# Group norm statistics from transposed y and ScalarE running sums; six depthwise-convolution taps moved behind the last turn

## The reference, cut to what matters

```
y = y * silu(z)                                        # 256 tokens x 256 channels of the group
yg = y * rsqrt(mean(y * y over the group's 256 channels) + 1e-6)
out = (yg * norm_g) @ out_w                            # summed over the groups
```

## Time and profile before

| | us |
|---|---|
| median of 3 runs | 915.81 |
| lowest and highest | 915.27, 915.85 |
| the profiled execution | 916.38 |
| its span in the trace | 914.6 |
| PE busy in the span | 903.7 |
| DVE busy | 757.4 |
| ACT busy | 560.1 |
| POOL busy | 18.3 |

### The profile page before, as it was taken

The page is one execution under the profiler, slowest core; times in us unless marked ns, Lnnn a source line. Parts: engine busy times, 40 slices in busy tenths (PEclk is TensorE's granted clock), DMA queues, the critical chain, the costliest instruction groups (busy, mean ns, idle before and its releaser), DMA issues.

```text
span 914.6 us, 18324 instructions
## 1 busy us (share of the span) xinstructions
PE 903.7 (99%) x6655; PEld 852.1 (93%) x6655; DVE 757.4 (83%) x1381; ACT 560.1 (61%) x954; POOL 18.3 (2%) x30
## 2 busy tenths in 40 slices
PE   9999999999999999999999999999999999999997
PEld 7999989999999999998888888999999999999886
DVE  5999999999999979689888646889979988888543
ACT  5649666776668474567666535579656766656432
POOL 1000000000000000000000000100000000000000
PEclk9999999999999999999999999999999999999999
DMA  9577235635346537537655554455437455555601
GB/s 329 178 269 228 97 116 183 202 128 197 137 163 207 207 94 278 183 117 251 199 186 187 186 185 163 143 179 186 153 132 264 147 195 179 181 180 180 230 1 46
DMA packets 45630, 161.56 MB, mean 177 GB/s; under 512 B 5348, under 2 KB 6024, under 8 KB 45448
## 3 DMA queue, kind: packets, MB, share of 16 engines
q1 hardware_dynamic: 43488, 154.74, 50.2%
q10 hardware_dynamic: 2088, 6.08, 1.8%
HBM read 159.72 MB, written 1.09 MB: 176 GB/s over the span
## 4 chain that ended last, share of the span: by engine, by line
PE 58%; issue 25%; DVE 13%; ACT 2%; DMA 1%; POOL 0%; SPq 0%; DVEq 0%; POOLq 0%; ACTq 0%
PE A L446 8%; PE A L447 7%; PE A L448 7%; PE B L665 5%; DVE w_lo L1347 4%; PE A L475 4%; PE B L475 3%; PE B L446 2%; PE B L447 2%; PE B L448 2%; PE A L477 2%; DVE part L1383 2%; PE B L477 2%; PE B L746 2%; PE A L746 1%
## 5 line engine op out<-in xcount | busy, mean ns | idle before, releaser
L1347 DVE TENSOR_TENSOR w_lo<-raw,w_hi 128x1024 fp32r<-128x1024 f32 x269 | 326.1, 1220 | 66.5 <-ACT w_hi L897 65.0
L897 ACT ACTIVATE w_hi<-raw 128x1024 fp32r<-128x1024 f32 x269 | 280.2, 1052 | 70.2 <-PE A L747 20.9
L446 PE MATMUL A<-h,w_hi 128*128 128x256 f32 x952 | 273.8, 288 | 0.2 <-DVE sc L1961 0.2
L447 PE MATMUL A<-h,w_hi 128*128 128x256 f32 x952 | 269.2, 283 | 0.0
L448 PE MATMUL A<-h,w_lo 128*128 128x256 f32 x952 | 269.2, 283 | 0.0
L446 PEld LDWEIGHTS A<-h,w_hi 128*128 128x128 f32 x952 | 182.1, 191 | 3.2 <-issue 2.6
L447 PEld LDWEIGHTS A<-h,w_hi 128*128 128x128 f32 x952 | 182.3, 192 | 0.1
L448 PEld LDWEIGHTS A<-h,w_lo 128*128 128x128 f32 x952 | 182.1, 191 | 0.0
L446 PE MATMUL B<-h,w_hi 128*128 128x256 f32 x352 | 100.1, 284 | 0.0
L447 PE MATMUL B<-h,w_hi 128*128 128x256 f32 x352 | 99.6, 283 | 0.0
L448 PE MATMUL B<-h,w_lo 128*128 128x256 f32 x352 | 99.6, 283 | 0.0
(11 more groups left out here) (308 smaller groups left out, 1575.5 us busy)
## 6 DMA issues: line engine op xcount, KB each, us to landing
raw<-in_weights_dram SPq DMA_DIRECT2D x289, 512.0 KB, 4.3
csrow<-cs_dram ACTq DMA_DIRECT2D x9, 512.0 KB, 4.5
x<-in_x_dram SPq DMA_DIRECT2D x4, 256.0 KB, 4.7
bd<-in_lru_w_dram ACTq DMA_DIRECT2D x1, 1024.0 KB, 6.2
out_dram<-m_wide SPq DMA_DIRECT2D x3, 256.0 KB, 2.1
raw<-in_weights_dram SPq DMA_DIRECT2D x2, 256.0 KB, 5.3
par<-in_params_dram SPq DMA_DIRECT2D x1, 379.0 KB, 6.8
out_dram<-m_wide ACTq DMA_DIRECT2D x2, 128.0 KB, 2.7
```

What stands on the lines that cost most here:

```text
L446: mm(dst, wh, lo, start=first, stop=False, skip_group_check=free)
L447: mm(dst, wh, hi, start=False, stop=False, skip_group_check=free)
L897: F(w_hi[:, s, :], raw[:, s, :], ACT.Copy).then_inc(hi_ready, 1)
L1347: V.tensor_tensor(w_lo[:, s, :], raw[:, s, :], w_hi[:, s, :].bitcast(F32), ALU.subtract).then_inc(lo_ready, 1)
```

## The change

The sums of squares are made another way. TensorE transposes the four 128 x 128 blocks of `y` into `A[3]` (tokens then on partitions), ScalarE squares each half of 128 x 256 out of PSUM with a running sum along the row (`accum_out`) into the new tile `ysum`, and `y_mean` reads `ysum` in SBUF. In the turns g = 1 to 7 the transposes stand in the middle of the second `out_piece`, after four of its eight matmuls; in the first turn they stand where `y_sums` stood. ScalarE's order changes with it. Three taps each of the channel tiles 0 and 1 (taps 24 to 26) leave the first turn and are made right after the last one. In the first and the last turn `y_mean` now comes ahead of the `w_lo` split beside it.

```diff
-            def y_sums(g):
-                pe.wait_ge(ysq_ready, g + 1)
+            def y_transposes(g):
+                pe.wait_ge(yz_ready, g + 1)
                 for t in range(TT):
                     for c in range(2):
-                        ins = mm(sums[:, t:t + 1], ysq[:, c, t * P:(t + 1) * P], ones[:, 0:1],
-                                 start=c == 0, stop=c == 1)
-                ins.then_inc(sums_ready, 1)
+                        ins = nc.tensor.transpose(A[3][:, t * T + c * P:t * T + (c + 1) * P], y[:, c, t * P:(t + 1) * P],
+                                                  ident)
+                ins.then_inc(yt_ready, 1)
...
-            def out_piece(p, turn, g, c):
+            def out_piece(p, turn, g, c, between=None):
                 native_loaded(p, turn)
                 pe.wait_ge(scale_read, g + 2)
                 for m in range(KD):
+                    if between is not None and m == KD // 2:
+                        y_transposes(between)
...
-            chain = {1: cb, 2: x_transposes, 3: y_products, 4: y_sums, 5: y_scale}
+            chain = {1: cb, 2: x_transposes, 3: y_products, 5: y_scale}
...
-                        out_piece(base + OUT_AT[s // 4], t, g - 1, s // 4)
+                        out_piece(base + OUT_AT[s // 4], t, g - 1, s // 4, g if s == 4 else None)
...
-            first_chain = {1: cb, 3: x_transposes, 5: y_products, 7: y_sums, 8: y_scale}
+            first_chain = {1: cb, 3: x_transposes, 5: y_products, 7: y_transposes, 8: y_scale}
...
             def y_squares(g):
-                act.wait_ge(yz_ready, g + 1)
-                F(ysq[:, :, :], y[:, :, :], ACT.Square).then_inc(ysq_ready, 1)
+                act.wait_ge(yt_ready, g + 1)
+                for t in range(TT):
+                    ins = F(ysq[:, t, :], A[3][:, t * T:(t + 1) * T], ACT.Square, accum_out=ysum[:, t:t + 1])
+                ins.then_inc(sums_ready, 1)
...
                 split(6)
+                act.wait_ge(cb_used, g + 1)
+                first_taps(g + 1, (0, 1))
+                act.wait_ge(yz_ready, g + 1)
+                first_taps(g + 1, (2, 3))
                 y_squares(g)
-                first_taps(g + 1)
...
                     if n == 6:
+                        act.wait_ge(yz_ready, 1)
+                        first_taps(1)
                         y_squares(0)
-                        first_taps(1)
...
-            GLU_TAPS, LOOP_TAPS, LATE_TAPS = range(5), range(5, CONV_K - 4), range(CONV_K - 4, CONV_K)
+            GLU_TAPS, LOOP_TAPS, LATE_TAPS = range(5), range(5, CONV_K - 7), range(CONV_K - 4, CONV_K)
+            LAST_TAPS = range(CONV_K - 7, CONV_K - 4)
...
-                moment_of(g + 2, 2 * P, RMS_EPS).then_inc(mean_ready, 1)
+                moment_of(g + 2, 2 * P, RMS_EPS, ysum[:, :]).then_inc(mean_ready, 1)
...
-                lo()
-                y_mean(g)
+                if looped:
+                    lo()
+                    y_mean(g)
+                else:
+                    y_mean(g)
+                    lo()
...
             group_turn(g, ahead(GATES0, 8), GATES0 + OUT_AT[1] + 1, more=False)
+            late_taps((0, 1), LAST_TAPS)
             for n in range(8, GATE_AT[-1] + 1 - LEAD):
```

More of the change, by code:

```diff
@@ L223, in hybrid_kernel @@
         dt_parts = ysq[:, 0, :]
+        ysum = sb("ysum", [P, TT], scope=s3)
         s3.close()
@@ L340, in hybrid_kernel @@
         dec_ready, m_ready, y_ready, yz_ready = sem("dec_ready"), sem("m_ready"), sem("y_ready"), sem("yz_ready")
-        ysq_ready, first_tap = sem("ysq_ready"), sem("first_tap")
+        yt_ready, first_tap = sem("yt_ready"), sem("first_tap")
         conv_operand_ready, mixed_ready = sem("conv_operand_ready"), sem("mixed_ready")
@@ L690, in _ @@
                 if s in (1, 4):
-                    out_piece(GATES0 + OUT_AT[s // 4], 0, g - 1, s // 4)
+                    out_piece(GATES0 + OUT_AT[s // 4], 0, g - 1, s // 4, g if s == 4 else None)
                 if s in chain:
@@ L965, in ring, with first_taps @@
                 return A[o % 3][:, 0:T]
-            def first_taps(g):
+            def first_taps(g, js=range(4)):
                 act.wait_ge(drained, drained_by(g, 3))
                 dyn = not isinstance(g, int)
-                for j in range(4):
+                for j in js:
                     at = (g * 4 + j) * SSM_K + SSM_K - 1
@@ L1601, in y_normed, with late_taps @@
                 ins.then_inc(scale_read, 1)
-            def late_taps(cs):
+            def late_taps(cs, ks=LATE_TAPS):
                 last = {c: own.value() for c in cs}
-                for k in LATE_TAPS:
+                for k in ks:
                     for c in cs:
```

## The result

| | before | after |
|---|---|---|
| median, us | 915.58 | 916.88 |
| lowest and highest, us | 914.9, 916.03 | 916.31, 917.5 |
| the profiled execution, its span | 916.38, 914.6 | 916.67, 914.9 |

The ratio is 1.0015 (95% interval 1.0009 to 1.0021), from 20 runs of each: the change makes the kernel 1.3 us slower. That is inside the 1.8 us that the prediction called "within 0.2%", and inside its range, but the forecast of -1.84 us has the wrong sign.

What follows compares the result with a forecast made beforehand. The prediction took TensorE as the bound, busy 903.7 of 914.6 us. Loop -2.76, first turn +1.0 and tail -0.08 made -1.84 us, from a median of 915.81 to 914.0 us; range 910.6 to 917.4.

Steps and rivals of the forecast that it cites:

- TensorE's own work, 0.46 us a turn: In every turn, four transposes (0.35 us) replace the sums' matmul group (0.81 us): 0.46 us less, bounds 0.3 to 0.8.
- The squares: ScalarE's two squares per turn, with running sums: 0.75 us for both, bounds 0.5 to 1.5 us.
- rival D: TensorE's clock falls because transposes don't count as activity: +12 us, 926 us; chance 0.02.
- rival B: Slow squares make ScalarE the bound: at 2.0 us for two, +4.1 us, 919.9 us; chance 0.10.
- The first turn, +1.0: ScalarE's squares wait for TensorE's transposes, so the loop begins 1.0 us late; bounds +0.75 to +1.75.
- rival A: ScalarE doesn't hold the first turn: -5.4 us, 910.4 us; 913.1 if only the tail is better; chance 0.19 with better tail.
- The loop, -2.76: In the loop and its first part, six turns (g = 1 to 6) each gain TensorE's 0.46 us: -2.76 us.
- the 27.8: Loop period in us above which the prediction called itself wrong; it expected 27.6.
- Rival C: VectorE or the loads, late by 0.43 us, hold the loop turn: +0.9 us, 916.7 us; chance 0.15.
- The tail, -0.08: Last turn and behind: TensorE's gain goes into waiting at the layer norm's sum behind six taps; -0.08 us, bounds -1.0 to +0.5.

Runs made afterwards that it cites:

- Experiment 3: Changed kernel with the first turn's transposes of y behind the seventh piece instead of the eighth: 914.85 us, ratio 0.9990.
- experiment 6: Changed kernel with the six moved taps back in the first turn: 915.69 us, ratio 1.0001.
- experiment 5: Kernel before the change, with only the six taps moved from the first turn behind the last: 914.86 us, ratio 0.9992.
- six memsets, not counted: Changed kernel with six small VectorE memsets added in the first turn, not raising VectorE's own semaphore: 915.68 us, ratio 1.0002.
- experiment 9: Changed kernel with the first turn's transposes behind the seventh piece and the mean ahead of VectorE's split in every turn: 912.74 us, ratio 0.9967.
- before, late mean: Kernel before the change, with the mean made two taps later in the loop turns: 921.86 us, ratio 1.0065.
- experiments 6 to 8: Changed kernel with the six taps back in the first turn (915.69 us), or six memsets added there, uncounted (915.68 us) or counted by VectorE's semaphore (915.89 us).
- experiment 2: Changed kernel with the mean directly ahead of VectorE's split in the loop turns too: 914.87 us, ratio 0.9991.
- experiment 1: Changed kernel with the mean made between the taps in the loop turns, two taps ahead of VectorE's split: 915.44 us, ratio 0.9998.

## Why the prediction was wrong, by its own steps

**TensorE's own work, 0.46 us a turn: right.** Transposes in the cut `out_piece` take 161.92 - 161.48 = 0.44 us of starts, not 0.35, but what stands behind them starts sooner by about as much; the turn up to the scale is 0.45 us shorter. The squares were inside their bounds: from the first square to the table load 0.85 us, a pair being 0.37 us from start to start (0.75 for two in the prediction). The granted clock stayed at 1.00, so rival D fell; rival B too, with 0.37 us a square.

**The first turn, +1.0: right, +1.02.** Each sign is there: ScalarE's wait of 1.92 us for the transposes, VectorE's of 3.33 for the split, TensorE's of 1.70 for the gate drain and 1.33 for `dec` (forecast 1.5 to 2). With that rival A fell. Experiment 3 moves the one instruction group that was blamed and gets 2.00 us back; experiment 6 shows that the taps have no part in it, though with the old sums they gain 1.15 us (experiment 5). The chain was read rightly. What was not drawn from it is that the cure was one number in a table.

**The loop, -2.76: the step that failed.** In its words: "GpSimd ends at 165.76 and TensorE, 0.46 us earlier, comes to L547 at 165.93 [...]: 0.15 us of slack, no wait." (The two times differ by 0.17.) No wait is printed at L548, but the time is lost behind it, and the period of 28.06 us lies above the 27.8 that the prediction named as the sign of being wrong. Set GpSimd's end against the start of the scale and of the next turn's first matmul, which stands behind the loop's back edge:

| kernel | GpSimd ends | scale starts, later by | next turn's first matmul, later than GpSimd's end by |
|---|---|---|---|
| before | 165.76 | 0.63 | 0.77 |
| before, taps moved | 164.29 | 0.51 | 0.65 |
| mean before split | 221.31 | 0.43 | 0.63 |
| taps back | 166.13 | 0.17 | 0.64 |
| six memsets, not counted | 165.80 | 0.17 | 0.64 |
| experiment 9 | 219.01 | 0.43 | 0.68 |
| after | 166.45 | 0.07 | 0.64 |
| before, late mean | 225.79 | 0.06 | 0.63 |

However the scale comes, the next turn's first matmul starts 0.63 to 0.68 us behind GpSimd's end in seven of these kernels (0.62 to 0.69 in their turns g = 2 to 5), and not sooner; only before, which has time to spare, shows more. The next matmul follows the scale after 0.13 to 0.14 us when nothing holds it, so the scale needs a lead of 0.5 us. Before had 0.63, that is 0.13 us of real slack and not the 0.63 that the rows seemed to show; the change asked for 0.46.

That the back edge has a part in it, the same instructions show where there is no jump back. On the last pass, g = 6, which leaves the loop, the next matmul starts 0.40 us behind GpSimd's end in after (0.39 in before, late mean; 0.41 in taps back), and in the last turn, which is written out, 0.24 us. The reading that fits is that TensorE's sequencer runs ahead of the array, so that its waits and the jump back are normally done before the array gets there, and that a scale which comes late stops it ahead of the jump. No row shows the sequencer itself. The Trainium skill says as much of the running ahead ("TensorE: Matmul & The Clock Gate", Part 2, step ⑤ NX overlap: the sequencer pops the next instruction without waiting for the array to drain). The 0.64 us are measured here; that the stopped sequencer is their cause is argued, not shown.

The second part of the same term: the chain to GpSimd's start should not have moved, and it came 0.12 us later (13.71 us behind the transposes, before 13.59). That is VectorE's 0.27 us in place of 0.16 ahead of y, shown in experiments 6 to 8 to come from there being six instructions fewer in the stream ahead of the loop. Together: 13.71 + 0.85 + 0.64 = 15.20 us from the transposes to the next turn, and before needed 15.22 for TensorE's own work. The period could only stay.

**Rival C** gave 916.7 and the median is 916.88, but its mechanism, "VectorE or the loads late by 0.43 us", is not what happened: with the mean moved ahead of one split, the period falls to 27.68 with the same loads and the same VectorE work (experiment 2), and in the changed kernel's turn g = 2 VectorE still waits for TensorE, 0.29 us before L1571 and 0.48 us before L1576. VectorE's work from the transposes to the mean is a part of the chain that held, so the rival came nearer than the forecast; but what that chain lacked was the lead at the back edge. That VectorE's slack is thin was right, as experiment 1 shows. Rivals B and D fell, as said above.

**The tail, -0.08: roughly right in sum, wrong in its parts.** From `cb` of g = 7 to the layer norm's sum the change is 0.05 us shorter. But the scale's wait didn't go: the mean came a split earlier, at 305.21, and GpSimd took 1.59 us beside that split in place of 0.86, so TensorE still stands before L548, from one start to the next 0.75 us (before 0.68). The prediction set 0.86 for every power, from the one row where taps of 0.4 us run beside it. The trace of before has a power of the other kind, in a later stage, beside a split:

```profile
329.10 1.21 DVE L1347 TENSOR_TENSOR w_lo<-raw,w_hi 128x1024 fp32r<-128x1024 f32 x1
```

```profile
329.26 1.60 POOL L422 TENSOR_TENSOR scale<-moment,half 128x2 f32<-128x2 f32 x1 [22.10 <-DVE moment L1357]
```

TensorE, held before L548, comes late to L702 and waits 0.18 us there, not 0.8. The Trainium skill has the rule that was missed ("SBUF — State Buffer", Who interferes with whom): a VectorE instruction with two inputs in SBUF contends with a GpSimd instruction that reads SBUF, because its second input comes through the read interface that the two share. The traces agree: 1.6 us beside a split of 1.2, 0.85 to 0.98 beside taps of 0.4 to 0.5. They don't show that the power is blocked for the whole of the split: in the last turn of after 1.05 us of the split are left when the power starts, and the power grows by 0.73.

**The sum.** +1.0 (first turn) + 0.4 (the first pass through the loop: VectorE's wait ahead of y is 0.52 us there in place of 0.16, GpSimd starts 0.28 us later behind the transposes, and the next matmul follows its end 0.10 us later) - 0.3 (the last pass, which leaves the loop and doesn't jump back) - 0.05 = +1.05 against the forecast's -1.84; the medians say +1.3. Nearly all of the error is one term, the -2.76 us of the loop, which came out at +0.1. That the time still fell inside the stated range, and on rival C's number, is luck: the term that was meant to make up for the first turn gave nothing, and the range was wide enough to hold that.

## What to carry to other kernels

A wait that stands ahead of a loop's back edge can need a lead, here 0.5 us: measure its slack not where the array starts the waiting instruction but by the distance to the first instruction behind the jump, and count a faster engine's gain only up to that slack. Before a producer is made earlier, look at what will run beside it; a tiny GpSimd operation beside a long VectorE instruction with two inputs in SBUF can lose what the move won. And if one engine's queue is moved behind another's work (the squares behind TensorE's eighth piece), look first for an earlier place for that work.

## What the runs showed of the hardware that was not expected

- A wait ahead of a back edge: 0.62 to 0.69 us from GpSimd's end to the next turn's first matmul in seven kernels, with no idle time printed in after; about 0.4 us on the pass that leaves the loop.
- GpSimd's power on 128 x 2 f32 takes 0.85 to 0.98 us beside taps, 1.59 to 1.64 beside a split of 128 x 1024.
- A square of 128 x 256 out of PSUM with a running sum is two instructions, 0.38 and 0.20 us, and a pair starts 0.37 us after the pair before.
- The place of a loop in VectorE's instruction stream changes one wait in it, 0.27 against 0.16 us (0.52 against 0.16 in the first pass), and a wait behind it, 0.56 against 0.19; six memsets ahead of the loop make the kernel 1.1 to 1.2 us faster. Only the effect is shown, not its cause.
